# One layer of a hybrid mixer and expert-retrieval trunk: half of the sparse attention made between the expert weighings

## What is computed

```python
ya = dsa_attention(aq, ak, av, iq, ik, iw, ...)   # A: indexer scores, top 128 keys, 8 heads of 64, one shared k and v
yb = stick_breaking_attention(bq, bk, bv, ...)    # B
yc = gla_attention(cq, ck, cv, cr, ca, ...)       # C
gates = sigmoid(gl + b_gate)                      # 3 x 1024 columns
merged = gates[0]*(ya @ w_oa) + gates[1]*(yb @ w_ob) + gates[2]*(yc @ w_oc)
h = x + gate1 * (merged @ w_out)
...
# PEER, for each token: 8 heads, each the best 16 of 16384 experts by product keys
u, vv = u_tab[expert], v_tab[expert]
act = gelu(einsum('nd,nhkd->nhk', xb, u))
h = h + gate2 * einsum('nhk,nhkd->nd', g * act, vv)
```

## Time and profile before

| | |
|---|---|
| median of 3 runs | 2109.4 us (2108.7 to 2110.21) |
| profiled execution: its own time, its span | 2111.97 us, 2110.2 us |
| TensorE, weight loads | busy 1780.4 us (84%), 992.2 us (47%) |
| VectorE, ScalarE, GpSimd | busy 1329.2, 571.8, 751.9 us |
| granted TensorE clock, mean | 0.944 |
| DMA | 657.44 MB, mean 312 GB/s |

### The profile page before, as it was taken

The page is one execution under the profiler, slowest core; times in us unless marked ns, Lnnn a source line. Parts: engine busy times, 40 slices in busy tenths (PEclk is TensorE's granted clock), DMA queues, the critical chain, the costliest instruction groups (busy, mean ns, idle before and its releaser), DMA issues.

```text
span 2110.2 us, 18198 instructions
## 1 busy us (share of the span) xinstructions
PE 1780.4 (84%) x5914; PEld 992.2 (47%) x5914; DVE 1329.2 (63%) x3162; ACT 571.8 (27%) x1318; POOL 751.9 (36%) x555
## 2 busy tenths in 40 slices
PE   4998999999988899999989987888788766676676
PEld 3443456566778665555555533444344322222222
DVE  4128543366732776666667787677666777777765
ACT  2111132466422422222222223222222222222221
POOL 0146333011000343333323444544443544454441
PEclk8999899899999899999999988999889999899989
DMA  8231124002233999999999999999999999999996
GB/s 362 77 128 80 80 80 170 0 31 90 75 118 117 398 419 419 419 420 419 419 407 385 419 420 387 417 419 420 420 419 421 419 420 419 420 420 420 419 420 251
DMA packets 87871, 657.44 MB, mean 312 GB/s; under 512 B 9680, under 2 KB 9696, under 8 KB 14432
## 3 DMA queue, kind: packets, MB, share of 16 engines
q0 software_dynamic: 73728, 536.90, 61.6%
q1 hardware_dynamic: 13888, 119.11, 14.1%
q10 hardware_dynamic: 160, 0.26, 0.1%
HBM read 653.88 MB, written 2.10 MB: 311 GB/s over the span
## 4 chain that ended last, share of the span: by engine, by line
PE 46%; DMA 38%; DVE 6%; issue 5%; ACT 4%; POOL 1%; SPq 0%; DVEq 0%; POOLq 0%; ACTq 0%
DMA sb<-uv_table,sb 36%; PE ps L1016 15%; PE ps L594 6%; PE ps L596 3%; PE ps L701 3%; PE ps L911 3%; PE ps L715 2%; PE ps L939 2%; PE ps L962 1%; PE ps L944 1%; PE ps L877 1%; POOL sb L1941 1%; DMA sb<-w_mod 1%; PE ps L737 1%; DVE sb L1784 1%
## 5 line engine op out<-in xcount | busy, mean ns | idle before, releaser
L1016 PE MATMUL ps<-sb 128*128 128x512 f32 x1792 | 875.3, 637 | 238.9 <-ACT sb L1325 235.1
L1941 POOL DMA_INDIRECT sb<-uv_table,sb x512 | 597.9, 1168 | 888.8 <-PE ps L1016 723.0
L1784 DVE CUSTOM_DVE_ANT_0 sb<-sb 128x1024 f32<-128x1024 f32 x512 | 627.0, 1225 | 378.3 <-DMA sb<-uv_table,sb 376.1
L1016 PEld LDWEIGHTS ps<-sb 128*128 128x128 f32 x1792 | 347.7, 202 | 729.7 <-issue 386.8
L1325 ACT ACTIVATE sb<-sb 128x128 f32<-128x128 f32 x448 | 158.8, 395 | 613.8 <-DVE sb L1793 611.4
L1314 ACT ACTIVATE sb<-sb 128x2 f32<-128x2 f32 x256 | 51.6, 201 | 409.6 <-DVE sb L1784 409.6
L594 PE MATMUL ps<-sb 128*128 128x512 f32 x304 | 137.0, 603 | 0.0
L911 PE MATMUL ps<-sb 128*128 128x256 f32 (+1 forms) x608 | 120.8, 354 | 6.2 <-DMA sb<-w_pq 5.9
L1898 POOL TENSOR_SCALAR sb<-sb 128x4096 f32<-128x4096 f32 x6 | 63.7, 10616 | 174.4 <-DMA sb<-w_mod 174.4
L911 PEld LDWEIGHTS ps<-sb 128*128 128x128 f32 x608 | 104.6, 198 | 32.1 <-issue 15.6
L701 PE MATMUL ps<-sb 128*128 128x256 f32 x384 | 92.0, 393 | 4.9 <-DVE sb L1622 2.8
(11 more groups left out here) (248 smaller groups left out, 1846.1 us busy)
## 6 DMA issues: line engine op xcount, KB each, us to landing
sb<-w_mod SPq DMA_DIRECT2D x12, 2048.0 KB, 10.0
sb<-w_pq SPq DMA_DIRECT2D x19, 1152.0 KB, 10.5
sb<-w_merge SPq DMA_DIRECT2D x24, 768.0 KB, 8.5
sb<-w_proj SPq DMA_DIRECT2D x8, 2048.0 KB, 12.9
sb<-w_merge SPq DMA_DIRECT2D x6, 2304.0 KB, 8.8
sb<-uv_table,sb POOLq DMA_INDIRECT x512, 20.9
sb<-w_merge SPq DMA_DIRECT2D x3, 1536.0 KB, 6.4
sb<-w_out SPq DMA_DIRECT2D x4, 1024.0 KB, 9.7
```

The source lines that it names most:

```text
L1016: mm = pe.matmul(bank(2 * (t % 2) + f), dgw[m % NDG], row_v(n)[:, T * f:T * (f + 1)], start=(i == 0), stop=(i == PH * PK - 2))
L1784: dve.tensor_tensor_reduce(out=row_u(n), in0=row_u(n), in1=n2_tm(u // PH), scale=1.0, scalar=0.0, op0=ALU.mult, op1=ALU.add, accum_out=dot ...
L1941: pool.indirect_dma_start(out=ring[PLACE[n]], out_offset=None, in_=uv_table, in_offset=bass.IndirectOffsetOnAxis(ap=experts[u % 4][:, i:i ...
```

## The change

Query tiles 2 and 3 of branch A (tokens 256 to 511, 16 of the 32 heads) are no longer made in the attention loop, which now has `NF` = 16 iterations. Their inputs (keys, two tiles of queries, two penalties, 1.2 MB) are written to a DRAM tensor `kept` by five DMAs of ACT. SP reads them back with two DMAs, after the first three `merge_weights` and ahead of `query_weights(2)`, into the memory of ring places 8 and 9. One head is then made per slot, its steps spread over slots j to j+4. Places 8 and 9 join the ring at row 108, and their first gathers wait for the last turn of A. The projection jobs stand after every second head; `mod2` blocks all use place 0 and projections places 1 and 2. Merges go B, C, A. Scores of queries move from PSUM bank 5 to 4. `gate_row` moves to slot 28 and `to_tokens(6, 7)` to slot 25.

```diff
-    order = [("mod1", i) for i in range(KT // 2)] + [("proj", 0)]
-    for i in range(KT):
-        order += ([("proj", i + 1)] if i + 1 < KT else []) + [("mod2", i)]
-    stream = [(kind, i, n % NSLOT) for n, (kind, i) in enumerate(order)]
+    stream = [("mod1", i, i % NSLOT) for i in range(KT // 2)] + [("proj", 0, 1), ("proj", 1, 2), ("mod2", 0, 0), ("proj", 2, 1), ("mod2", 1, 0)]
+    for i in range(2, KT):
+        stream += ([("mod2", i, 0)] if i == 2 else []) + ([("proj", i + 1, 1 + (i + 1) % 2)] if i + 1 < KT else [])
+        stream += [("mod2", i, 0)] if i > 2 else []
...
-            free = list(range(10))
+            free = list(range(R_EARLY))
...
+                if n == KEPT_UNTIL:
+                    free = [8, 9] + free
...
+        def half_unit(n):
+            return (n // KT + 1) % 3, n % KT
+
+        def late_at(j):
+            return 1 + j + (3 if j >= HA else 0)
+
+        LATE_SCORE = {late_at(j): j for j in range(NF)}
+        LATE_SUM = {late_at(j) + 2: j for j in range(NF)}
+        LATE_TURN = {late_at(j) + 3: j for j in range(NF)}
+        LATE_PROD = {late_at(j) + 4: j for j in range(NF)}
+        LATE_OUT = {late_at(HA * i + HA - 1) + 6: 2 + i for i in range(2)}
+        LATE_Y = {late_at(HA * i + HA - 1) + 7: 2 + i for i in range(2)}
...
-        TURN_SLOT = {2: (6, 7), 46: (8, 9), 48: (10, 11), 53: (12, 13), 54: (14, 15)}
-        G2_SLOT = 15
+        TURN_SLOT = {25: (6, 7), 46: (8, 9), 48: (10, 11), 53: (12, 13), 54: (14, 15)}
+        G2_SLOT = 28
...
+            sp.wait_ge(s["kept_out"], 5 * 16)
+            sp.dma_start(area("w", KEPT, 3 * T), kept[:, 0:3 * T]).then_inc(s["kept_in"], 16)
+            sp.dma_start(area("w", late + T, 896), kept[:, 3 * T:3 * T + 896]).then_inc(s["kept_in"], 16)
             query_weights(2)
...
-        MOD_AT = (31, 33)
+        MOD_AT = (14, 16)
...
-            return J_A + it // 3 if it % 3 == 1 and J_A + it // 3 < NJ - LATE else None
+            return J_A + it // 2 if it % 2 == 1 and J_A + it // 2 < NJ - LATE else None
...
+            def late_scores(j):
+                qt, h = 2 + j // HA, j % HA
...
+                pe.wait_ge(s["la_read"], NF + j)
+                pe.matmul(bank(2, n), q_h(qt)[r:r + HD, h // 2, :], ka_h[r:r + HD, 0:n], start=True, stop=True)\
+                  .then_inc(s["la_done"], 1)
+            def late_turn(j):
+                pe.wait_ge(s["prob_ready"], NF + j + 1)
+                pe.wait_ge(s["pt_out"], NF + j)
...
+                for st in range(2 + j // HA + 1):
+                    mm = pe.transpose(bank(3, P, P * st), prob_h(j)[:, P * st:P * (st + 1)], ident)
...
+            def late_output(qt):
+                pe.wait_ge(s["o_ready"], qt + 1)
+                for f in range(4):
+                    mm = pe.transpose(bank(5, P, P * f), o_h[:, P * f:P * (f + 1)], ident)
+                mm.then_inc(s["ot_done"], 1)
+            def amid(slot):
+                if slot in LATE_PROD:
+                    late_product(LATE_PROD[slot])
+                if slot in LATE_TURN:
+                    late_turn(LATE_TURN[slot])
+                if slot - 1 in LATE_OUT:
+                    late_output(LATE_OUT[slot - 1])
...
                 for n in range(max(EARLY, GROUP * slot), GROUP * (slot + 1)):
+                    if n % GROUP == 2:
+                        amid(slot)
                     if not on_dve(n):
                         weigh(n)
+                if slot in LATE_SCORE:
+                    late_scores(LATE_SCORE[slot])
...
-            NA = TT * HA
+            act.wait_ge(s["ka_twice"], 16)
+            act.dma_start(kept[:, 0:T], ka).then_inc(s["kept_out"], 16)
...
+            NA = NF
...
+                if slot in LATE_SUM:
+                    late_exp(LATE_SUM[slot])
                 if part == 1 and u + 1 < NU:
                     exponents(u + 1)
+                if slot in LATE_SUM or part == 1:
                     act.activation(warm, cact[:, 0:1], ACT.Gelu)
...
+            dve.wait_ge(s["kept_out"], 5 * 16)
...
+            def late_sum(j):
...
+                dve.wait_ge(s["la_done"], i + 1)
+                dve.wait_ge(s["pt_done"], i - 1)
...
+                if i % 4 == 1 and n // GROUP in LATE_SUM:
+                    late_sum(LATE_SUM[n // GROUP])
+                if i % 4 == 1 and n // GROUP in LATE_OUT:
+                    late_out(LATE_OUT[n // GROUP])
...
                 elif R_EARLY <= PLACE[n] < 10:
-                    pool.wait_ge(s["yo_done"], 4)
+                    pool.wait_ge(s["ot_done"], TT)
```

More of the change, by code:

```diff
@@ L258, in n2_tm, with q_h, pen_h, prob_h @@
             return area("vb", D * t, D) if t < 2 else area("w", D * (t - 2), D)
+        KEPT = 4608
+        ka_h = area("w", KEPT, T)
+        late = KEPT + 3 * T
+        o_h = area("w", late, T)
+        def q_h(qt):
+            return tiles(area("w", late + T if qt == 2 else KEPT + 2 * T, T), 4)
+        def pen_h(qt):
+            return area("w", late + 2 * T, 3 * P) if qt == 2 else area("w", KEPT + T, T)
+        def prob_h(j):
+            return area("w", late + 1408 + 384 * (j % 2), 384) if j < HA else area("w", late + T * (1 + j % 2), T)
+        def probT_h(j):
+            return area("w", late + 2176, 384) if j < HA else area("w", late + 2048, T)
+        def amax_h(j):
+            return area("stat", 64 + j % HA, 1)
+        NF = (TT // 2) * HA
         NU = TT * PH
@@ L1018, in weigh, with late_product @@
                 mm.then_inc(s["weighed"], 1)
+            def late_scores(j):
+                qt, h = 2 + j // HA, j % HA
+                r, n = HD * (h % 2), P * (qt + 1)
+                if j == 0:
+                    pe.wait_ge(s["kept_in"], 32)
+                    pe.wait_ge(s["nvar_ready"], 2)
+                pe.wait_ge(s["la_read"], NF + j)
[4 more added lines that the diff above has]
+                pe.wait_ge(s["pt_out"], NF + j)
+                if j == 0:
+                    pe.wait_ge(s["tm_out"], 6)
+                for st in range(2 + j // HA + 1):
+                    mm = pe.transpose(bank(3, P, P * st), prob_h(j)[:, P * st:P * (st + 1)], ident)
+                mm.then_inc(s["pt_done"], 1)
+            def late_product(j):
+                qt, h = 2 + j // HA, j % HA
+                pe.wait_ge(s["pt_out"], NF + j + 1)
+                if j == 0:
+                    pe.wait_ge(s["yg_ready"], 4)
+                if j == HA:
+                    pe.wait_ge(s["ot_out"], 3)
+                for st in range(qt + 1):
+                    mm = pe.matmul(bank(5, HD, HD * h), probT_h(j)[:, P * st:P * (st + 1)], va[:, st, 0:HD],
+                                   start=(st == 0), stop=(st == qt))
+                mm.then_inc(s["pv_done"], 1)
+            def late_output(qt):
[10 more added lines that the diff above has]
+                    late_output(LATE_OUT[slot - 1])
             for n in range(EARLY):
@@ L1277, in half_gate @@
                     act.wait_ge(s["gate_used"], NG + n - 1)
-                act.activation(gates_h[n % 2], bank(6, H), ACT.Tanh, scale=0.5, bias=half_bias[:, n:n + 1])\
+                br, c = half_unit(n)
+                act.activation(gates_h[n % 2], bank(6, H), ACT.Tanh, scale=0.5, bias=half_bias[:, KT * br + c:KT * br + c + 1])\
                    .then_inc(s["gate_ready"], 1)
@@ L1326, in diagonals, with late_exp, late_copy, late_y @@
                        .then_inc(s["dg_ready"], 1)
+            def late_exp(j):
+                act.wait_ge(s["nmax_ready"], NF + j + 1)
+                p, i = prob_h(j), NF + j
+                act.activation(p, p, ACT.Exp, bias=anmax[:, i:i + 1], accum_out=asum[:, i:i + 1]).then_inc(s["prob_ready"], 1)
+            def late_copy(j):
+                act.wait_ge(s["pt_done"], NF + j + 1)
+                act.wait_ge(s["pv_done"], NF + j)
+                act.activation(probT_h(j), bank(3, P * (3 + j // HA)), ACT.Copy).then_inc(s["pt_out"], 1)
+            def late_y(qt):
+                act.wait_ge(s["ot_done"], qt + 1)
+                act.activation(y_of(0, 1)[:, :, P * (qt % 2):P * (qt % 2 + 1)], tiles(bank(5), 4), ACT.Copy).then_inc(s["ot_out"], 1)
             exponents(0)
@@ L1339, in _ @@
                 u, part = divmod(slot, 4)
+                if slot in LATE_PROD:
+                    late_copy(LATE_PROD[slot])
+                if slot - 1 in LATE_Y:
+                    late_y(LATE_Y[slot - 1])
                 for pair in range(max(EARLY // 2, 2 * slot), 2 * slot + 2):
@@ L1494, in _ @@
                     dve.tensor_scalar(anmax[:, it:it + 1], amax[:, it:it + 1], -1.0, None, ALU.mult).then_inc(s["nmax_ready"], 1)
-                if it % 3 == 1 and it // 3 < HA:
+                if it % 2 == 1 and it < NA:
                     top_keys(3, TOPK // 64)
-                    if it // 3 == HA - 1:
+                    if it == NA - 1:
                         penalty(3)
+                        dve.sem_inc(s["pen_ready"], 1)
                 if it >= 3 and (it - 3) % HA == HA - 1:
```

54 lines of the change are left out of this document (40 added, 14 removed).

## The result

| | before | changed |
|---|---|---|
| median of 4 runs each | 2109.81 us (2108.7 to 2111.25) | 2127.85 us (2123.71 to 2129.02) |
| ratio, 95% interval | | 1.007 (1.0058 to 1.0082) |
| profiled execution, its span | 2111.97 us, 2110.2 us | 2127.64 us, 2125.8 us |
| TensorE, VectorE, ScalarE busy | 1780.4, 1329.2, 571.8 us | 1784.2, 1334.0, 604.9 us |

The account below looks back on a forecast made before the run. It took a serial 689 us front, then a stream bound by DMA at 420 GB/s with TensorE close to its limit. Terms: 2112.0 - 25 + 1 + 31 + 10 = 2129 profiled, median 2126 us, range 2100 to 2145.

Parts of the forecast that it names:

- The front: what goes, and block 7: Attention loop: moved heads save 38.1 us, waiting for w_mod block 7 costs 12.4; front 25 us shorter (22 to 37).
- The front ahead of the loop: Start up to 231.5 us, before the attention loop: taken as unchanged, 0 us.
- Between front and stream: Reading back 1.25 MB ahead of query_weights(2), for which TensorE waits: 0 to 3 us, taken as +1.
- The stretch: Slot 1 to row 105: TensorE's added work and waits lengthen it by 31 us (20 to 45).
- handshakes: New handshakes in three places of each slot of the stretch: 0 to 15 us, taken as 3.
- the start: Start of the stretch: two places fewer take away rows landed ahead, 3 us (0 to 5).
- Places 8 and 9: Rows 106 to 108: row 108's gather waits for A's last turn and pauses the stream, 10 us (8 to 13).
- ScalarE: ACT in the stretch: 54 us of new work including table loads, off the path, costing 0.
- Gaps take the heads: Rival, faster: TensorE's gaps absorb moved heads, stretch grows 0 to 5 us instead of 31, total 2098; chance 0.18.
- The blocks are in time: Rival, same time: block 7 doesn't hold DVE, front gives 37 us, total 2114; chance 0.14.
- Eight places starve the stream: Rival, much slower: eight places give a row per 3.5 us, total 2166; chance 0.10.
- three signs of being wrong: Stretch grows by less than 15 us, row 108's gather costs no pause, or DVE finds block 7 landed.

Follow-up runs that it names:

- e4: Changed kernel with block 7 of mod2 added at iterations 17 and 18 instead of 14 and 16: 2111.17 us, ratio 0.9996.
- e5: Kernel before with only the new order and places of SP's weight loads: 2127.02 us, ratio 1.0072.
- e2: Kernel before with the ring on eight places until row 114, nothing else changed: 2114.16 us, ratio 1.001.
- e1: Changed kernel with places 8 and 9 joining the ring at row 114 instead of 108: 2114.9 us, ratio 1.0013.
- e9: Changed kernel with the edits of e1 and e4, plus GpSimd holding block 1 until first head factors are made, block 4 until branch B's last query/key scaling: 2088.62 us.

## Why the prediction was right in its sum, and where it was wrong

**The front: what goes, and block 7.** Right in mechanism and nearly in size, 15 us later than forecast. DVE is idle 14.36 us on `w_mod` up to 325.64 (8 to 10 forecast), and head 14 waits 11.57 us (12.4 forecast); block 6 went from issue to GpSimd in 12.4 us (12.9) and block 7 reached DVE 7.6 us after GpSimd was done with block 6 (7.45). The 3 us between -25 and -21.9 are mostly the job behind that wait, 9.45 us instead of 7.1. I priced the wait as idle time alone; on this chip it also costs the clock behind it. e4 gives the whole: 14.5 us. Without the wait, the loop of e4 is 142.1 - 105.7 = 36.4 us shorter than before, where 38.1 - 0.7 = 37.4 was forecast.

**The front ahead of the loop.** This is the step that failed. The prediction held the front up to 231.5 as unchanged, since no instruction was added or taken there. Its own row had the warning: GpSimd's passes of 10.62 and 8.85 us stood in it as a cost of the blocks only, never beside what DVE does meanwhile. The change moves them. With the 15.3 us the front is 6.6 us shorter and not 25, and branch B begins at 368.81, not near 350. The first gather is at 677.02 where I said near 665: what the front lost, less the next item.

**Between front and stream.** +1 was forecast and -6.3 measured. From branch B's first matmul to the first weighing it is 339.5 us before and 333.2 changed. The windows behind branch B's start show the clock, first before, then changed:

```profile
375.45:500.00 124.55, 116.31 (x417) 75.35 (x418) 62.97 (x94) 69.04 (x65) 17.56 (x21) 0.92 0.09 32
```

```profile
368.81:500.00 131.19, 120.48 (x468) 79.78 (x469) 71.68 (x108) 77.28 (x72) 22.27 (x25) 0.99 0.11 40
```

Branch B's first matmuls took 4.63 us before and in e5, and 2.39 us in every kernel whose loop has 16 heads. But e2, with the old loop, also takes 333.2 us, and e5 336.6. In the other seven kernels with the short loop it is 329.8 to 334.4. So a part of the 6 us belongs to the one execution that I made the sum against, and a part may come from a loop that ends at a higher clock; no run parts the two.

**The stretch.** The cause was right (TensorE, at 98.9%), the term of 31 us was too large by 12.3. The sum of TensorE's busy time was 4.7 too large: it grew by 310.10 - 280.26 = 29.8 us, not 34.5. Of the two output turns only one lies in the stretch, and it takes 0.44 us (893.20 to 893.64) instead of 0.6; the other stands at 1031.60, just behind it. Where the rest of the 4.7 went is not shown: the two heads that I had measured have no idle time in them. And of the 10.9 us of waits that I set on top, TensorE shows 3.5: handshakes 0.5 (ahead of L1072) instead of 3, the 1.9 ahead of merges gone, and nothing visible for the start. TensorE's idle time fell from 14.6 to 3.5 us: once 30 us of new work made it the bound, that work filled its gaps. The low end of that step was 20, and it came out at 18.7, outside the step's own range.

**Places 8 and 9.** Right in place, mechanism and size: +9.9 against 10, of which e1 returns 9.3. POOL's and DVE's timelines of the changed kernel:

```profile
1032.47 0.94 POOL L2098 DMA_INDIRECT sb<-uv_table,sb  x1 [19.07 <-PE ps L1102]
```

```profile
1038.28 1.23 DVE L1937 CUSTOM_DVE_ANT_0 sb<-sb 128x1024 f32<-128x1024 f32 x1 [11.72 <-DMA sb<-uv_table,sb]
```

The gather is issued 0.3 us behind the turn, dotted 5.8 us later, and weighed at 1040.07: TensorE stands 7.88 us (8 to 9 forecast). The page of the Trainium skill weighed there (DMA: Bandwidth & Descriptors, "Anatomy of one DMA") gave an estimated 4.4 us for such a transfer; these 5.8 us, issue and semaphore included, lie between it and my 6.2.

**ScalarE.** Its busy time in the stretch grew from 74.6 to 125.28 us, by 50.7 (54 forecast), and TensorE waits 0.9 us for its diagonals instead of 10.4: 0 on the path, as forecast. VectorE's grew by 8.1 us (15 forecast), also off the path.

**The rivals.** "Gaps take the heads" had the right reason in small (11 of 14.6 us of gaps filled) but TensorE had no 30 us to give. "The blocks are in time" is e4, and its 2114 is near the 2111 measured. "Eight places starve the stream" is refuted by e2. None of the three signs of being wrong that the prediction named appeared; none of them looked at the front ahead of the loop.

## To carry to other kernels

When a change reorders loads, list what each landing starts on GpSimd, and set those spans against VectorE's instructions with two SBUF inputs and its TENSOR_SCALARs from SBUF to SBUF: here that cost 15 us of front (e5 has 14.2, e9 gives 13.4 back), with no instruction added. Such a hold shows as a long duration, not as a wait, so compare the same instruction's duration in two traces. And where a ring gets memory late, let its first use lie well behind the release in the order of the queue, so that no later gather waits with it (row 114 instead of 108 cost nothing and saved 9 us).

## What the runs showed of the hardware

- A multiplication of 16x512 from SBUF takes 0.68 us alone and up to 9.24 us beside a GpSimd pass over 128x4096; three held instructions ended 0.54 or 0.55 us after the pass. In e5 a TENSOR_SCALAR of 16x512 is held likewise (8.91 us instead of 0.42). The end isn't always so near: before, a SCALAR_TENSOR_TENSOR ends at 162.85 beside a TENSOR_SCALAR pass that ends at 164.18.
- TensorE's granted clock fell after short idle times: 2.5 us of idle at 108.8, then 0.67 over 111 to 125 us and jobs of 9.67 and 9.88 us instead of 7.15; 7.88 us of idle at 1032, then 0.64 over the window 1031.6 to 1046. e9, without the first of these idle times, has 1.00 there. Traffic of DMA isn't needed for it: behind the wait of 11.57 us the clock is 0.50 over 329.2 to 332 us with no DMA moving. A clock of 1.2 GHz for part of the time costs more after the first of them (7.6 us) than the idle time itself.
- The profiles of the kernels with the new order and without waits of GpSimd, all alike up to the loop, begin it between 243.7 and 248.6 us, so the 15.3 us above are the upper end of 10.3 to 15.3. The likely reason is that where a GpSimd pass falls against a VectorE instruction differs a little from execution to execution, and a hold or a clock step makes microseconds of it. A term of one profiled execution carries such an uncertainty.
- Eight places of 1 MB gave 413 GB/s (e2), ten 419.
